# Norm rows spread by PE from a column, the last square summed by PE, a join begun beside the embedding's products, operands at multiples of 512 bytes

## The reference, cut to what matters

```python
def rms_norm(x, g):
    return x * rsqrt(mean(x * x, axis=-1) + EPS) * g

# first block
mod = silu(c) @ w_ada + b_ada                     # shifts, scales and gates
h = rms_norm(x, norm_mix_g) * (1 + sc1) + sh1
proj = h @ w_in + b_in                            # convolution, mLSTM, gates
...                                               # layer_norm ahead of w_conv_pw
x = x + g1 * (merged @ w_out)
h = rms_norm(x, norm_ffn_g) * (1 + sc2) + sh2
x = x + g2 * ((silu(gt) * up) @ w_ffn_down)       # gt, up = h @ w_ffn_up
x = rms_norm(x, final_norm_g)
# second block
xn = rmsnorm(h, pre_mix_norm)
mix = token_mixer(xn, ...)                        # retention and latent attention
h = h + rmsnorm(mix, post_mix_norm)
ff = (silu(hn @ w_gate) * (hn @ w_up)) @ w_down   # hn = rmsnorm(h, pre_ffn_norm)
h = h + rmsnorm(ff, post_ffn_norm)
e = rmsnorm(p @ w_ple_proj, ple_norm)
h = h + e * sigmoid(h @ w_ple_gate + b_ple_gate)
```

## Time and profile before

| | |
|---|---|
| median of 3 runs | 1706.56 us (1702.82 to 1707.67) |
| the profiled execution | 1704.14 us, its span 1702.2 us |
| granted TensorE clock, mean | 0.977 |
| PE busy | 1617.2 us, 95% |
| DVE busy | 1022.8 us, 60% |
| ACT busy | 623.3 us, 37% |
| HBM read | 167.48 MB, 101 GB/s over the span |

### The profile page before, as it was taken

One profiled execution on the slowest core, in us unless ns is written; L12 is line 12 of the kernel. 1 busy time (PEld: TensorE's weight loads), 2 busy tenths in 40 slices (PEclk: granted clock), 3 DMA queues, 4 the chain that ended last, 5 costly groups with the idle time before them and its releaser, 6 DMA issues.

```text
span 1702.2 us, 18384 instructions
## 1 busy us (share of the span) xinstructions
PE 1617.2 (95%) x7176; PEld 1312.4 (77%) x7176; DVE 1022.8 (60%) x1527; ACT 623.3 (37%) x881; POOL 114.1 (7%) x94
## 2 busy tenths in 40 slices
PE   5999898999999899999999998999989999999988
PEld 4887776778778788888888886778867888888867
DVE  6699888889668644333464447766566444442255
ACT  3221465654442342222233233546453222222223
POOL 0000000000000000000011001000142111100010
PEclk9999988999899899999999999999999999999999
DMA  9133221222446334233332321211332333333332
GB/s 357 50 99 104 70 74 63 62 75 87 148 173 210 100 122 141 96 96 92 92 108 82 116 78 61 82 44 38 98 101 87 95 93 98 99 93 96 96 112 74
DMA packets 48191, 172.87 MB, mean 102 GB/s; under 512 B 5349, under 2 KB 5477, under 8 KB 47849
## 3 DMA queue, kind: packets, MB, share of 16 engines
q1 hardware_dynamic: 48104, 171.70, 31.6%
HBM read 167.48 MB, written 4.19 MB: 101 GB/s over the span
## 4 chain that ended last, share of the span: by engine, by line
PE 83%; DVE 11%; ACT 3%; issue 2%; DMA 0%; POOL 0%; SPq 0%; DVEq 0%; POOLq 0%; ACTq 0%
PE bank L1329 24%; PE bank L1330 24%; PE bank L1337 23%; DVE tmp L1874 1%; PE bank L1349 1%; DVE spl L1723 1%; PE bank L1351 1%; PE bank L1350 1%; DVE convout L1808 1%; PE bank L1432 1%; PE bank L1415 1%; PE bank L1445 1%; DVE XT L2211 1%; PE bank L1365 1%; ACT tmp L1498 1%
## 5 line engine op out<-in xcount | busy, mean ns | idle before, releaser
L1329 PE MATMUL bank<-HH,sph 128*128 128x512 f32 x1480 | 600.7, 406 | 28.9 <-DVE spl L1723 11.3
L1330 PE MATMUL bank<-HH,spl 128*128 128x512 f32 x1480 | 588.3, 397 | 0.0
L1723 DVE TENSOR_TENSOR spl<-raw,sph 128x1024 fp32r<-128x1024 f32 (+1 forms) x261 | 330.9, 1269 | 316.9 <-ACT sph L1490 316.5
L1337 PE MATMUL bank<-HL,sph 128*128 128x512 f32 x1480 | 385.9, 395 | 0.9 <-DVE HL L2215 0.9
L1329 PEld LDWEIGHTS bank<-HH,sph 128*128 128x128 f32 x1480 | 284.5, 192 | 100.6 <-issue 26.9
L1490 ACT ACTIVATE sph<-raw 128x1024 fp32r<-128x1024 f32 (+1 forms) x261 | 269.6, 1034 | 216.0 <-PE bank L1337 166.1
L1330 PEld LDWEIGHTS bank<-HH,spl 128*128 128x128 f32 x1480 | 285.0, 193 | 59.9 <-issue 1.4
L1337 PEld LDWEIGHTS bank<-HL,sph 128*128 128x128 f32 x1480 | 280.1, 190 | 63.2 <-DVE HL L2215 2.2
L1808 DVE SCALAR_TENSOR_TENSOR convout<-convin,vecs,convout 128x512 f32<-128x512 f32 x240 | 166.7, 745 | 0.0
L1329 PE MATMUL bank<-midh,sph 128*128 128x512 f32 x352 | 138.7, 394 | 0.0
L1330 PE MATMUL bank<-midh,spl 128*128 128x512 f32 x352 | 138.7, 394 | 0.0
(11 more groups left out here) (294 smaller groups left out, 1567.7 us busy)
## 6 DMA issues: line engine op xcount, KB each, us to landing
raw<-in_w_in SPq DMA_DIRECT2D x73, 512.0 KB, 3.6
raw<-in_w_up SPq DMA_DIRECT2D x66, 512.0 KB, 3.6
more<-in_w_ada SPq DMA_DIRECT2D x32, 512.0 KB, 4.5
raw<-in_w_down SPq DMA_DIRECT2D x32, 512.0 KB, 3.5
raw<-in_w_gate SPq DMA_DIRECT2D x22, 512.0 KB, 3.6
ada<-in_w_ada SPq DMA_DIRECT2D x16, 512.0 KB, 14.6
raw<-in_w_down SPq DMA_DIRECT2D x16, 384.0 KB, 3.1
raw<-in_w_v SPq DMA_DIRECT2D x8, 512.0 KB, 3.6
```

Source lines behind the costliest of these rows:

```text
L1329: e.matmul(P_[b][:], sph(n)[:, q], hi[:, k, :], start=k == 0, stop=False)
L1330: e.matmul(P_[b][:], spl(n)[:, q], hi[:, k, :], start=False, stop=False)
L1337: m = e.matmul(P_[b][:], sph(n)[:, q], low[:, k, :], start=False, stop=last and k == kb - 1)
L1723: e.tensor_tensor(spl(n), raw(n), sph(n).bitcast(F32), ALU.subtract).then_inc(*up("s_w_low", ("wl", n)))
```

## The change

Four edits.

- `spread`: the diagonal tiles of DVE are gone. PE takes the column itself, repeated along a row by a zero step, as weights, and the identity as the moving operand.
- `SumSq.add(..., last=True)`, for the last tile of x1, mix and ff: its square goes to a buffer of its own and is not added; `columns_two` has PE multiply both the running sum and this square with the ones, into the same columns. The add of tile 7 of x1, of mix and of ff leaves DVE.
- Between the embedding's products: the spread of mix comes after the fifth product instead of the sixth, behind a `ready(more=1)` that cuts and loads a weight unit there; joins 0, 1 and 2 of mix come after products 5, 6 and 7.
- Addresses: `base` is 16896, `B` is rounded up to a multiple of 512, `ah` and `al` move by 64. `XT`, `HH`, `HL`, `raw`, `sph`, `spl`, everything placed at a multiple of 512 from `B`, and `ah`, `al` then start at 0 modulo 512.

```diff
@@ -294,9 +294,13 @@
         def __init__(self, name):
             self.name, self.n, self.t = name, 0, None
             self.a, self.free = tmp.take()
-
-        def add(self, src, after, scale=None, eng="dve"):
-            if self.n == 0:
+            self.j = None
+
+        def add(self, src, after, scale=None, eng="dve", last=False):
+            if last:
+                self.j, free = tmp.take()
+                add("square", self.name, self.n, self.j, free, src, after, scale)
+            elif self.n == 0:
                 add("square", self.name, 0, self.a, self.free, src, after, scale)
                 self.t = ("sq", self.name, 0)
             else:
@@ -310,7 +314,11 @@
 
         def columns(self):
             b, bfree = misc.take()
-            add("columns", self.name, self.a, b, bfree, self.t)
+            if self.j is None:
+                add("columns", self.name, self.a, b, bfree, self.t)
+            else:
+                add("columns_two", self.name, self.a, self.j, b, bfree, self.t, ("sq", self.name, self.n - 1))
+                tmp.give(self.j, ("cols", self.name))
             tmp.give(self.a, ("cols", self.name))
             return b
 
@@ -320,10 +328,8 @@
         return r
 
     def spread(name, src, after):
-        i, free = tmp.take()
         b, bfree = misc.take()
-        add("spread", name, src, i, free, b, bfree, after)
-        tmp.give(i, ("rows", name))
+        add("spread", name, src, b, bfree, after)
         return b
 
     def root_of(ss, width):
@@ -684,7 +690,7 @@
     def out_evac(i):
         def evac(b, g):
             add("out", i, b, g)
-            ss.add(("XT", i), [("x", 1, i)])
+            ss.add(("XT", i), [("x", 1, i)], last=i == 7)
             return [("x", 1, i)]
         return evac
 
@@ -985,20 +991,29 @@
 
     def branch(name, i, ss):
         def evac(b, g):
-            after = ss.add(("bank", b), [("tile", g)], eng="pool" if i < 7 else "dve")
+            after = ss.add(("bank", b), [("tile", g)], eng="pool", last=i == 7)
             add("branch", name, i, b, after)
             return [("branch", name, i)]
         return evac
 
-    def join(name, b, then, later):
+    def join_in_turn(name, b, then, later):
         def first(i):
             j, free = tmp.take()
             add("join", name, i, b, j, free)
             tmp.give(j, ("x", {"MIXO": 4, "FFO": 5}[name], i))
             then(i)
 
-        in_turn(8, first, later)
+        for i in range(9):
+            if i < 8:
+                first(i)
+            if i:
+                later(i - 1)
+            yield
         misc.give(b, ("join", name, 7))
+
+    def join(*args):
+        for _ in join_in_turn(*args):
+            pass
 
     ssm, sse = SumSq("mix"), SumSq("e")
     gemms([("w_o", i, branch("MIXO", i, ssm), (lambda: add("p_cut")) if i == 3 else None) for i in range(8)], "mix")
@@ -1013,18 +1028,22 @@
     for i in range(3):
         e_products[i]()
     r = root_of(ssm, D)
-    for i in range(3, 6):
+    for i in range(3, 5):
         e_products[i]()
+    ready(more=1)
     b = spread("mix", ("small", r), [("rs", "mix")])
-    e_products[6]()
-    e_products[7]()
     ss = SumSq("x4")
 
     def pf_later(i):
         add("pf_lo", i)
         ss.add(("XT", i), [("x", 4, i)], eng="pool")
 
-    join("MIXO", b, lambda i: add("pf_hi", i), pf_later)
+    joined = join_in_turn("MIXO", b, lambda i: add("pf_hi", i), pf_later)
+    for i in range(5, 8):
+        e_products[i]()
+        next(joined)
+    for _ in joined:
+        pass
     add("e_spill")
     fence("f2")
     ecol = keepc(4)
@@ -1079,7 +1098,7 @@
         def each(labels):
             return [at(*label) for label in labels]
 
-        base = 16512
+        base = 16896
 
         def place(name, off, shape, dt=F32):
             return nc.alloc_sbuf_tensor_at(name, shape, dt, offset=base + off)
@@ -1100,16 +1119,17 @@
         KEEP = place("kept", o, [128, 176]); o += 704
         MOD = place("mod", o, [128, 48]); o += 192
         XP = place("xpad", o, [128, 2, 516])
-        TRIG = place("trig", o, [128, 4, S]); o += 4128
-        MORE = [place("more0", o - 4128, [128, 1024]), place("more1", o + 4128, [128, 1024])]
+        TRIG = place("trig", o, [128, 4, S]); o += 4224
+        MORE = [place("more0", o - 4224, [128, 1024]), place("more1", o + 4224, [128, 1024])]
         ACC = place("modacc", o, [128, 1024])
         SPH.append(place("sph_first", o, [128, 1024], F32R))
-        SPL.append(place("spl_first", o + 4128, [128, 1024], F32R))
-        SPH.append(place("sph_second", o - 4128, [128, 1024], F32R))
-        HT = place("htok", o, [128, 4, 258]); o += 4128
+        SPL.append(place("spl_first", o + 4224, [128, 1024], F32R))
+        SPH.append(place("sph_second", o - 4224, [128, 1024], F32R))
+        HT = place("htok", o, [128, 4, 258]); o += 4224
         MROW = place("mrow", o, [4, S]); o += 2048
         RROW = place("rrow", o, [128, S]); o += 2048
         TMP = [place(f"tmp{i}", o + 2048 * i, [128, S]) for i in range(NT)]; o += 2048 * NT
+        o += -(base + o) % 512
         B = o
         MH = place("midh", B, [128, NFT, S], F32R)
         ML = place("midl", B + NFT * 2048, [128, NFT, S], F32R)
@@ -1127,8 +1147,8 @@
         ADA = [place(f"ada{i}", B + 17344 + 4096 * i, [128, 2, 512]) for i in range(16)]
         IR, LF, BR, CR = [place(f"row{i}", B + 50176 + 2048 * i, [4, S]) for i in range(4)]
         ROWC = place("rowc", B + 66560, [4, 10, 128])
-        AH = place("ah", B + 33728, [128, 8, S], F32R)
-        AL = place("al", B + 33728 + 16384, [128, 8, S], F32R)
+        AH = place("ah", B + 33792, [128, 8, S], F32R)
+        AL = place("al", B + 33792 + 16384, [128, 8, S], F32R)
         QH = place("qh", B, [96, 8, S])
         CQ = place("cq", B, [128, 3, S])
         CKV = place("ckv", B + 6144, [128, 2, S])
@@ -1358,11 +1378,20 @@
                     m = e.matmul(P_[b][:, t:t + 1], TMP[a][:, token(t)], ONES[:, 0:1], start=True, stop=True)
                 m.then_inc(*up("s_column", ("cols", name)))
 
-            def spread(name, src, i, free, b, bfree, after):
-                w.wait_ge(at("ones"), *each(bfree))
+            def columns_two(name, a, j, b, bfree, after, last):
+                w.wait_ge(at(*after), at("ones"), *each(bfree))
                 for t in range(T):
-                    w.wait_ge(at("diag", name, t))
-                    m = e.matmul(P_[b][:, token(t)], ONES[:], TMP[i][:, token(t)], start=True, stop=True)
+                    e.matmul(P_[b][:, t:t + 1], TMP[a][:, token(t)], ONES[:, 0:1], start=t == 0, stop=False)
+                w.wait_ge(at(*last))
+                for t in range(T):
+                    m = e.matmul(P_[b][:, t:t + 1], TMP[j][:, token(t)], ONES[:, 0:1], start=False, stop=t == T - 1)
+                m.then_inc(*up("s_column", ("cols", name)))
+
+            def spread(name, src, b, bfree, after):
+                r = columns_of(src, T)
+                w.wait_ge(*each(after), at("consts"), *each(bfree))
+                for t in range(T):
+                    m = e.matmul(P_[b][:, token(t)], r[:, t:t + 1].broadcast_to([128, 128]), IDENT, start=True, stop=True)
                 m.then_inc(*up("s_rows", ("rows", name)))
 
             def columns_of_pair(p):
...
@@ -1734,13 +1763,6 @@
                     *up("s_scale", ("rs1", name)))
                 w.wait_ge(at("rs2", name))
                 e.reciprocal(sm(r, n), sm(q, n)).then_inc(*up("s_scale", ("rs", name)))
-
-            def spread(name, src, i, free, b, bfree, after):
-                r = columns_of(src, T)
-                w.wait_ge(*each(after), *each(free), at("consts"))
-                for t in range(T):
-                    e.tensor_scalar(TMP[i][:, token(t)], IDENT, r[:, t:t + 1], None, ALU.mult).then_inc(
-                        *up("s_scale", ("diag", name, t)))
 
             def mod_sum(p, first, last, acc):
                 wide = TMP[acc[0]][:]
...
```

More of the change, by code:

```diff
@@ L2242, in pg @@
                 e.tensor_tensor(XT[:, i, :], XT[:, i, :], TMP[j][:], ALU.add).then_inc(*up("s_x", ("x", 6, i)))
-            run({"split": split, "sum": total, "rsqrt": rsqrt, "spread": spread,
+            run({"split": split, "sum": total, "rsqrt": rsqrt,
                  "mod_sum": mod_sum, "mod_tiles": mod_tiles, "ada": ada, "ada_columns": ada_columns, "glu_mul": glu_mul, "tap": tap, "conv_sum": conv_sum, "v": v, "log_forget": log_forget, "decay": decay,
```

2 lines of the change are left out of this document (1 added, 1 removed).

## The result

The changed kernel takes 1679.65 us (median of 4 runs, 1678.44 to 1681.16) beside 1704.69 us of the kernel before (4 runs, 1702.62 to 1707.67): ratio 0.9852, 95% interval 0.9832 to 0.9872, about 25 us less. The forecast was 1682.7, 23.9 us less than the 1706.56 at which the kernel before stood then. The profiled span is 1676.6 us (before 1702.2), the mean granted clock 0.981 (before 0.977).

A forecast was written before the change was run, and what follows sets the result against it. PE was taken to bound the kernel, busy 95% of the span, the rest short holes waiting for norms, with DVE pacing the first join. Terms 1.0 + 1.4 + 1.5 + 7.0 + 5.0 + 7.0 + 1.0 = 23.9 off 1706.6 gave 1682.7 us, range 1645 to 1697.

The forecast's parts named there:

- Bare chains: Spreads at x0, x1 and ff: PE no longer waits for diagonal tiles, 0.34 us each, 1.0 us gained.
- last square: Norms of x1 and ff: the last add leaves the path, 2 x 0.7 = 1.4 us gained; mix covered by products.
- ln: Norm of ln: PE's wait of 1.46 us for diagonals made behind a weight split goes, 1.5 us gained.
- cq and kv: Norms of cq and kv: waits for diagonals and a half-clock drop go, 7.0 us gained, bounds 4 and 8.5.
- mix and the join: Spread of mix and first join: join starts 5.0 us earlier, DVE's pace unchanged, 5.0 us gained, bounds 1.6 and 5.6.
- Alignment of midh/midl: Down projections: 1056 products go from 233.3 to 226.7 ns by equal starts modulo 512, 7.0 us gained.
- a stage: AH/AL, 192 products moved from start 256 to 0: 0 to 1.3 us gained, taken as 1.0.
- HH/HL at 0 instead of 128: 4728 products, both starts moved by 128 and still equal: pitch stays 226.7 ns, gain 0; bounds 31.5 us either way.
- Rival B: HH/HL products: common start 0 lowers the pitch too, 31.5 us more gained, 1651 us; chance 22%.
- C: Rival: at common start 0 all HH products take 233.3 ns, midh no better; 1722 us, chance 9%.
- Rival D: Down projections: alignment does nothing, midh's upper-half place may cost the 6.67 ns; only waits go, 1690.7 us; chance 11%.
- A: The main forecast for the whole kernel, 1682.7 us, own range 1675 to 1692; chance 58%.

The follow-up runs named there:

- e3: Kernel before with only the last square of x1, mix and ff summed by PE alone, diagonal tiles kept; 1703.12 us, ratio 0.9989.
- e2: Kernel before with only the spread by a repeated column; 1693.67 us, ratio 0.9931 to the kernel before.
- second trace of after: A second profile of the same changed kernel; its lead over the kernel before is 22.1 us in all, 25.5 in the first profile.
- e4: Changed kernel with the old order of spread, weight cut and joins at mix; 1682.04 us, ratio 0.9864 to the kernel before.
- e1: Kernel before with only the new addresses; 1698.47 us, ratio 0.9959 to the kernel before.
- e9: Changed kernel with the cut weights, and all between them and `B`, 64 bytes further; 1707.58 us, ratio 1.0013 to the kernel before.
- e10: Changed kernel without POOL's seven adds of the squares of x4, so that norm is wrong; 1675.90 us, ratio 0.9836 to the kernel before.
- e6: Changed kernel without the weight unit cut and loaded ahead of the spread of mix; 1680.35 us, ratio 0.9851 to the kernel before.
- e5: Changed kernel with all eight joins of mix behind product 7, early cut kept; 1680.08 us, ratio 0.9849 to the kernel before.
- grid: Separate kernel, only PE at work: 32 groups of 48 fp32r products with varied moving and weights starts; 226.5 to 234.2 ns per product.
- e8: Changed kernel with everything from `B` on 256 bytes further; 1678.39 us, ratio 0.9853 to the kernel before.

## Why the prediction was right, point by point

- **What bounds the kernel.** Right: fewer nanoseconds per product count in full wherever PE is full, the rest is holes. The table's rows say the same place by place.
- **Bare chains, 1.0, and last square, 1.4.** Right in size. From the last square to the spread: x1 3.52 to 2.44 us, ff 3.46 to 2.41, 1.1 each for the two edits together, 1.04 forecast; e3 alone gave 0.76 at x1, and moved nothing at mix, where the sum had it covered. ff gained about 0.5 us more in the trace, since its spread ran partly at half clock before (1.73 us, now 1.25); that is luck, for in e2 it took 2.08. The allowance for the repeated column as weights was not needed: the spread takes what it took.
- **ln, 1.5.** Right: 1.6 us in the second trace of after. The 2.8 of the first, of e2 and of e4 holds more than the norm: the half-clock stretch ahead of ln lasted 6.8 us in these three and 10.2 in before and in the second trace of after.
- **cq and kv, 7.0.** Right, and step by step: both forecast times came out within 0.3 us, 7.5 us with the spread alone. The remaining 0.7 came with the addresses, which I had put at 0 here because DVE's waits cover it. Over products 3900 to 3950 the lead grows by 0.5 to 0.6 us in after, its repeat and e1, and not at all in e2. A half-clock stretch of 3.4 us lies there in before, e2, e3 and e9, and in no trace with equal starts, so part of this may be the clock's.
- **mix and the join, 5.0.** The step that was mis-sized. The first join came when forecast (4.8 us earlier), but 3.9 us arrived. I wrote that DVE's pace stays the old one, at 2.2 us a tile, and left POOL's adds to the lower bound. The 2.2 itself was misread: from the first join to the end of the eighth low half the eight tiles took 21.2 us before, 2.65 a tile. The stretch grew by 0.9 us, in two adds of the join that now fall beside adds of POOL, and e10 shows that such a loss is POOL's: its adds cost DVE up to 1 us for each instruction beside them, 3.6 us over the stretch for those of x4. That this stretch was DVE's was in the windows; that half a microsecond a tile of it was POOL's stood in the timeline of before, too. PE's first product behind the join waited 1.8 us, not the 1 us given as a sign.
- **Why the order gains.** Half right: e6 has the head start without the early cut, and e5 without the joins in between.
- **Alignment of midh/midl, 7.0.** Right: 5.44 us for 24 products, e1 7.0 us by its time. But the reason given, equal starts modulo 512, is too narrow: 0 against 256 is as good (grid, e8).
- **a stage, 1.0.** Wrong by its place: its products did go from about 232 to 227 ns, but the stage gained nothing (-0.2 us in both traces of after). Over products 1575 to 1750 the lead does grow by 0.9 us (e2: none), near the 1.0 forecast, and 0.8 of it is gone again 25 products later, behind the last product that reads `al`. So something else sets the end of the stage; what it is was not looked for.
- **HH/HL at 0 instead of 128.** Right: 226.7, gain 0. Rival B fell, C fell for this change; e9 shows that C's price was real, had the two starts come apart. Rival D fell with e1. The row used against D, weights from `sph_second` and `spl_second`, was weak. The fourteen products that took 230.0 ns take 233.6 in the changed kernel, with HH at 0, `sph_second` at 128 and `spl_second` at 0 modulo 512; by the grid (232 and 227 for these two differences) they would take 230. What holds them is open, as with the products that read kvh or kvl, which average 232 ns at equal starts.
- **The total.** It fits better than its terms, and that is partly luck: mix and the a stage gave 2.2 us less than forecast by the table, the rows of cq and kv and of the second up and down 1.7 more, and the rows ahead of product 2100 differ by 1.9 us between two traces of the same kernel. The range of A, 1675 to 1692, does not come out of the bounds named: these reach from 1680.3 (8.5, 5.6 and 1.3 in place of 7.0, 5.0 and 1.0) to about 1697 (4, 1.6 and 0, and 0.95 for each of seven spreads).

## What to carry to other kernels

In a stage that PE fills, read the distance between starts, not the duration, and compare streams of the same shape: here 3% hung on the difference of the start addresses of moving operand and weights modulo 256 bytes, and 64 bytes cost 27 us. Give all operands of the array starts with equal remainders modulo 256, at multiples of 32 or more, and keep padding between buffers from breaking that. Where a short step of one engine waits in line behind another engine's long list, as the diagonal tiles behind rope work, let the engine that needs the result do it; and where DVE paces a stage, look for adds of POOL beside it.

## What the runs showed of the hardware that was not expected

- The pitch of fp32r products of 512 columns goes by (moving start - weights start) modulo 256: 226.7 ns at 0, 229 at 64, 232 to 234 at the others tried, with nothing else running. The sign counts: +64 gives 229, -64 gives 233.
- Starts that are equal but at 16 bytes gave 231.0 ns, those at 32 bytes 227.1.
- A low-half step of DVE took 0.74 us alone and 1.77 beside an add of POOL, and POOL's add took 1.28 us at best and 1.77 beside DVE. A DVE step with one input in SBUF and one in PSUM was not slowed (0.67 to 0.68).
- The half-clock stretches (1.2 instead of 2.4 GHz) of one and the same kernel summed to 63 and 66 us within the span in two executions, and to 57 in that of e9.
